# Reordering one step of two attention passes: the earlier step's probabilities turned amid the keys, its values ahead of the scores, its exp first

## The reference

```
# second mixer (called dsa): 6 query heads on 2 key heads; the 256 best keys of each query are kept
logits = einsum('bqkgd,bqskd->bqkgs', qg, k_sel) * D_HEAD**-0.5
p = masked_softmax(logits + bias, valid)
o = einsum('bqkgs,bqskd->bqkgd', p, v_sel)
# sliding window (called win) of the third mixer: 512 rows of state_nsa_win per sequence
lw = einsum('bqkgd,bwkd->bqkgw', qg, win_k) * scale + grouped_bias(...)
o_win = einsum('bqkgw,bwkd->bqkgd', masked_softmax(lw, wmask), win_v)
```

## Time and profile before

| | us |
|---|---|
| median of three runs | 2874.64 |
| lowest, highest | 2871.42, 2877.35 |
| profiled execution | 2872.88 |
| its span in the trace | 2871.1 |
| dsa steps, first key turn to last sum | 2012.5 to 2193.6 |
| win steps, first key turn to last sum | 2204.8 to 2250.7 |

### The profile page before, as it was taken

One profiled execution on the slowest core, in us unless ns is written; L12 is line 12 of the kernel. 1 busy time (PEld: TensorE's weight loads), 2 busy tenths in 40 slices (PEclk: granted clock), 3 DMA queues, 4 the chain that ended last, 5 costly groups with the idle time before them and its releaser, 6 DMA issues. The chain is left out here.

```text
span 2871.1 us, 45368 instructions
## 1 busy us (share of the span) xinstructions
PE 2357.2 (82%) x16097; PEld 1786.6 (62%) x16097; DVE 1051.7 (37%) x1869; ACT 760.9 (27%) x1706; POOL 485.2 (17%) x335
## 2 busy tenths in 40 slices
PE   5999999999967989966588687884996544787996
PEld 3888888888867989963355344442554323665885
DVE  5101111101011222223488476664332279556213
ACT  3000000000011222210344345542553353344010
POOL 6433333333240000000000000000000000233431
PEclk7999999999979999979799799997998665898998
DMA  5333232332468786514899799995996630002223
GB/s 177 119 104 110 100 121 90 112 112 80 168 164 257 240 234 213 185 27 93 265 356 342 263 386 386 379 376 158 365 379 236 217 88 0 1 1 96 88 81 117
DMA packets 344412, 522.93 MB, mean 182 GB/s; under 512 B 67501, under 2 KB 150846, under 8 KB 341902
## 3 DMA queue, kind: packets, MB, share of 16 engines
q1 hardware_dynamic: 309722, 483.10, 50.3%
q10 hardware_dynamic: 31792, 32.05, 3.7%
q0 software_dynamic: 2704, 5.33, 0.6%
HBM read 498.09 MB, written 44.00 MB: 189 GB/s over the span
## 5 line engine op out<-in xcount | busy, mean ns | idle before, releaser
L461 PE MATMUL proj_acc<-proj_w_hi,h_hi 128*128 128x512 f32 (+1 forms) x960 | 369.9, 385 | 8.5 <-POOL proj_w_lo L430 8.5
L462 PE MATMUL proj_acc<-proj_w_hi,h_lo 128*128 128x512 f32 (+1 forms) x960 | 369.9, 385 | 0.0
L463 PE MATMUL proj_acc<-proj_w_lo,h_hi 128*128 128x512 f32 (+1 forms) x960 | 369.4, 385 | 0.0
L430 POOL TENSOR_TENSOR proj_w_lo<-w_in,proj_w_hi 128x2048 fp32r<-128x2048 f32 (+1 forms) x60 | 272.8, 4548 | 458.8 <-DVE proj_w_hi L399 458.8
L754 PE MATMUL cmp_hp<-cmp_xT,cmp_w 128*128 128x128 f32 x2048 | 253.1, 278 | 12.2 <-DVE cmp_xT L785 12.2
L399 DVE CAST proj_w_hi<-w_in 128x2048 fp32r<-128x2048 f32 (+1 forms) x60 | 81.1, 1356 | 465.9 <-PE proj_acc L454 463.1
L754 PEld LDWEIGHTS cmp_hp<-cmp_xT,cmp_w 128*128 128x128 f32 x2048 | 241.1, 194 | 16.3 <-DVE cmp_xT L785 15.9
L1250 PE MATMUL sb_tp<-kept_consts,sb_k_rows 128*128 128x128 f32 x1024 | 169.5, 315 | 64.1 <-DMA sb_k_rows<-in_cache_sb_kv_dram 47.9
L485 ACT COPY proj_out<-proj_acc 128x512 f32<-128x512 f32 (+1 forms) x60 | 34.7, 579 | 697.0 <-PE proj_acc L463 697.0
L1250 PEld LDWEIGHTS sb_tp<-kept_consts,sb_k_rows 128*128 128x128 f32 x1024 | 127.0, 158 | 136.8 <-ACT sb_kT L1390 63.0
L461 PEld LDWEIGHTS proj_acc<-proj_w_hi,h_hi 128*128 128x128 f32 x960 | 180.7, 188 | 44.3 <-issue 8.8
(11 more groups left out here) (407 smaller groups left out, 3583.6 us busy)
## 6 DMA issues: line engine op xcount, KB each, us to landing
cmp_rows<-in_cache_nsa_kv_dram SPq DMA_DIRECT2D x512, 128.0 KB, 2.4
slc_rows<-in_cache_nsa_kv_dram SPq DMA_DIRECT2D x256, 256.0 KB, 5.0
sb_k_rows<-in_cache_sb_kv_dram SPq DMA_DIRECT2D x256, 256.0 KB, 6.0
sb_v_rows<-in_cache_sb_kv_dram SPq DMA_DIRECT2D x256, 256.0 KB, 7.2
dsa_rows<-in_cache_dsa_kv_dram SPq DMA_DIRECT2D x256, 256.0 KB, 4.8
w_in<-in_w_in_dram SPq DMA_DIRECT2D x56, 1024.0 KB, 5.0
fin_w<-in_w_out_dram SPq DMA_DIRECT2D x32, 512.0 KB
proj<-proj_out ACTq DMA_DIRECT2D x14, 1024.0 KB, 4.3
```

What stands on the lines that cost most here:

```text
L430: pool.tensor_tensor(w_lo[q][:, :, 0:width], w[q][:, :, 0:width], w_hi[q][:, :, 0:width], ALU.subtract).then_inc(lo_made, 1)
L461: pe.matmul(to, h_hi[:, kk, r], w_hi[q][:, k, 0:width], start=(kk == 0), stop=False)
L462: pe.matmul(to, h_lo[:, kk, r], w_hi[q][:, k, 0:width], start=False, stop=False)
L463: last = pe.matmul(to, h_hi[:, kk, r], w_lo[q][:, k, 0:width], start=False, stop=(kk == KT_IN - 1))
```

## The change

A flag, `values_first`, is true for dsa and win. Where it is true, TensorE's order in a step becomes: turns of items 0 and 1, `turn_probs` of the earlier step, turns of items 2 and 3, `values` of the earlier step, `score`. ScalarE takes the earlier step's `exps` ahead of all four copies. No instruction is added or left out, and no semaphore, buffer or load is changed.

```diff
+    values_first = not stick and not rounds
@@ TensorE
-                    if not stick:
+                    if values_first:
+                        for j in range(items):
+                            if j == items // 2 and before(g, c):
+                                turn_probs(*before(g, c))
+                            turn(g, c, j)
+                        if before(g, c):
+                            values(*before(g, c))
+                        score(g, c, None)
+                    elif not stick:
                         for j in range(items):
                             turn(g, c, j)
...
-                    if before(g, c):
+                    if not values_first and before(g, c):
                         values(*before(g, c))
@@ ScalarE
-            when = {0: 0, 1: 1, 2: 2, 3: 8} if stick else {0: 1}
+            when = {0: 0, 1: 1, 2: 2, 3: 8} if stick else {0: -1} if values_first else {0: 1}
...
+                    if values_first and before(g, c):
+                        exps(*before(g, c))
                     for j in range(items):
                         copy_key(g, c, j)
```

## The result

The changed kernel takes 2883.94 us in the median of eight runs, against 2873.25 for the kernel before: a ratio of 1.0034, with a 95% interval from 1.0019 to 1.0049. It is slower by about 10 us. The two profiled executions differ by less in their spans, 2877.3 against 2871.1 us. The way from dsa's first scores to its last took 171.07 us before and 181.48 after, 10.4 more; win took 54.6 in both; and by the end of win the changed execution stood 9.5 us behind. The 3.3 that it won back came in later stages, which the change doesn't touch; executions of one kernel differ by more (2869.64 to 2880.89 before).

What follows compares the result with a forecast made beforehand. It took dsa to be bound by a ring of engines, not a queue of loads. dsa +10.3 us and win -2.2 (between -2.8 and -0.8) gave +8.1, rounded to +8.0: 2882.6 us from 2874.64, range 2875.5 to 2889.

Steps and rivals of the forecast that it cites:

- The step of dsa: dsa, scores to scores: 5.85 us in place of 5.547, over 30 steps 9.1 us.
- mask to scores: dsa, end of the step: time from mask matmul to scores, taken as 0.32 us, between 0 and 0.56.
- The first interval: dsa, first scores to second: 5.85 us in place of 4.67, +1.2, as values now stand in it too.
- rival 1: dsa: values and mask end before copy 3, step 5.3 until loads bind at 5.49; 2871.6 us in all; chance 0.14.
- load bound: dsa: 2.097 MB of loads a step at 382 GB/s allow no step under 5.49 us.
- A change of the array's shape: TensorE in dsa: each costs about 0.1 us, four a step in place of three, about 3 us over 31 steps.
- the third step's loads: win: the second step's values start 2.15 us earlier, and so do these loads, which wait for them.
- the gain of the third step's values: win: these values come earlier behind item 1's turn; 0.9 us gained, bounds 0.25 and 1.25.
- the late fourth scores: win, fourth step: scores now wait for values, 0.9 us lost, bounds 0.6 and 1.6.
- rival 3: win gives nothing, as the loads' pace or low clock takes it back: +10.3 us, 2884.9; chance 0.07.
- the mask's bounds: dsa: 31 times -0.32 or +0.24 us around +10.3, so +0.4 to +17.7.
- rival 4: dsa: longer waits cost TensorE its clock, a tenth of 31 steps at half pace, +14 us, 2896; chance 0.03.

## Why the prediction was right, point by point

**The step of dsa.** Every term on the path was met. From the scores, in the rows above: `limit` 1.13 (1.13), exp 1.93 (1.92), probabilities 2.79 (2.79), copies 2.83 (2.83), values 4.52 (4.54), mask 5.54 (5.53), scores 5.85 (5.85). The one term that no row of before showed, mask to scores, is 0.31 or 0.32; I had taken 0.32 between 0 and 0.56. That one has some luck in it: it rested on the next instruction starting 0.06 to 0.07 before the end of a group, which holds for probabilities and values in the rows, but not for scores, where it is 0.18 (2093.60 + 1.06 against 2094.48). At 0.18 the step would have come out 0.11 shorter. The first interval is 5.95, for 5.85. From first to last scores dsa grew by 10.4 us, for 10.3.

**Which edit costs.** I had put all of it on values and mask behind the last key turn. With values alone put back the interval is 5.27; exp first alone gives 5.28, the 5.3 of rival 1, and then its load bound, 5.49 by the prediction and 5.53 as measured from the ninth interval on. So rival 1's arithmetic was sound and its condition not met.

**A change of the array's shape.** I had said about 0.1 us each, four in a step in place of three. Removing one gave 0.14 a step (5.85 to 5.71), and the masks of slc and dsa differ by 0.10. The Trainium skill (TensorEngine Tiling (Array Packing), Key Properties) says that a change of tiling mode drains TensorE; the rows agree in so far as such a change costs time, with these numbers.

**The term that was mis-sized is win's.** I predicted -2.2. The first part of it, the third step's loads 2.15 earlier, came as 1.9. The other two hang on the clock: I took the gain of the third step's values as 0.9 and the late fourth scores as +0.9, both between the clock's two levels. In the profiled execution the gain was -0.3 (the fourth step's first turns came 1.6 earlier in all and its item 1 1.5, not 3.05) and the fourth scores, 5.2 behind their item 1's turns in place of 3.7, cost 1.5 for my 0.9. So win gave 0.0, which is rival 3's claim, to which I gave 0.07. In the kernel with win alone it gave 2.9. Over the profiles, those with TensorE's old order have stages of 54.6, 56.5, 55.5 and 55.1 us (the last two with exp first), those with the new one 54.6, 51.7 and 54.5: some 2 us less on average, about the size that I gave, and a spread as large, which I had too small. With three and four profiles such a mean is not shown to be the gain; it may be near 2.2 by luck.

**The sum.** +10.4 and -2 make +8, the measured ratio is +9.8 us with an interval from +5.5 to +14. The two agree, but so would +10.4 alone: what the forecast of the total owes to win can't be told from it. The range, 2875.5 to 2889, was said to cover the mask's bounds but for their outer thirds; by the prediction's own terms these bounds give 2872.8 to 2890.1, and it leaves out about a quarter of the lower part and a seventh of the upper.

**Clock in dsa (rival 4).** The clock stayed at 0.99, with TensorE idle 0.71 in the midst of every step.

## What to carry to other kernels

When two engines hand work around in a ring, walk the ring in the new order with durations and hand-over times of the old trace. Work that fills a wait is free where it stands; moved to between the last hand-over and the end of the ring, it costs what no other wait there covers, even when the move frees a buffer sooner. Here the values take 1.02 us with what follows, and their new place cost 0.57, as some 0.4 of them fall in what was a wait for the last copy. Look first at where an engine waits for loads: there the same work costs nothing and the buffer that it frees is worth most.

## What was not expected of the hardware

With exp first alone DMA moved 385 GB/s in the stretch from 2040 to 2100, was busy all the time, and bound the loop at 5.53 us a step; with half the bytes it was busy 0.68 of the time at 203 GB/s. The kernel before, at 382 GB/s and 5.55 us a step, was nearly at that bound, though no wait in its list shows it: a shorter ring alone could win little there. When loads bind, most steps take 5.4 us but about one in five takes 5.6 to 6.1; what these are is open. The low clock reached into win in every profile, not at the same place in each, and the same group of 32 matmuls took 1.08 us or 1.93 by it.
